# A three-block hybrid stack on one core: softmax start fused on VectorE, one attention step moved by a job, one weight split moved ahead of two squares

## The reference

```python
scores = einsum("bnqhgd,bnkhd->bhgnqk", qb, kb) * (HEAD_DIM ** -0.5)
scores = where(valid, scores + bias, NEG_INF)
m = maximum(max(scores, axis=-1, keepdims=True), sink_l)
p = exp(scores - m)
denom = sum(p, axis=-1, keepdims=True) + exp(sink_l - m)
p = p / denom
out = einsum("bhgnqk,bnkhd->bnqhgd", p, vb)
```

## Time and profile before

| what | value |
|---|---|
| median of three runs | 1438.81 us (1433.37 to 1439.4) |
| the profiled execution | 1435.38 us |
| its span, first to last instruction | 1433.6 us |
| mean granted TensorE clock | 0.985 |
| TensorE busy | 1364.9 us, 95% of the span |
| VectorE busy | 1027.4 us, 72% |
| ScalarE busy | 718.6 us, 50% |
| HBM read | 258.99 MB |

### The profile page before, as it was taken

How to read it: one execution, slowest core, us unless ns; L and a number is a source line. 1 busy time by engine, 2 the same in 40 slices (tenths; PEclk the granted TensorE clock), 3 DMA queues, 4 the chain that set the end, 5 groups by cost and what they waited for, 6 DMA issues and landing times. The chain is left out here.

```text
span 1433.6 us, 24250 instructions
## 1 busy us (share of the span) xinstructions
PE 1364.9 (95%) x9872; PEld 1260.0 (88%) x9872; DVE 1027.4 (72%) x1680; ACT 718.6 (50%) x1095; POOL 42.7 (3%) x80
## 2 busy tenths in 40 slices
PE   7999998999999999999998999999899999899996
PEld 6999997898999999999988989999778877889995
DVE  4487676776677664886777857777787986677775
ACT  5345657444443445446565443433468664545442
POOL 1000000000000000000000000000010000000000
PEclk9999999999999999999999999999999999999998
DMA  9964534463777654444444647677434313355450
GB/s 266 245 241 163 202 133 148 148 240 130 265 256 270 248 220 147 165 160 147 148 152 160 220 146 274 240 279 254 172 112 168 148 60 109 112 187 195 177 177 30
DMA packets 42152, 262.10 MB, mean 183 GB/s; under 512 B 5229, under 2 KB 5613, under 8 KB 14782
## 3 DMA queue, kind: packets, MB, share of 16 engines
q1 hardware_dynamic: 32688, 227.28, 45.5%
q0 software_dynamic: 9264, 33.24, 6.9%
q10 hardware_dynamic: 94, 0.07, 0.0%
HBM read 258.99 MB, written 1.58 MB: 182 GB/s over the span
## 5 line engine op out<-in xcount | busy, mean ns | idle before, releaser
L1608 DVE TENSOR_TENSOR split<-ring,split 128x1024 fp32r<-128x1024 f32 x412 | 487.3, 1220 | 204.8 <-ACT split L1165 203.9
L654 PE MATMUL psum<-h,split 128*128 128x256 f32 x2080 | 593.2, 285 | 6.9 <-DVE split L1608 6.4
L655 PE MATMUL psum<-h,split 128*128 128x256 f32 x2080 | 588.9, 283 | 0.0
L656 PE MATMUL psum<-h,split 128*128 128x256 f32 x2080 | 588.7, 283 | 0.0
L1165 ACT CAST split<-ring 128x1024 fp32r<-128x1024 f32 x411 | 410.5, 1047 | 254.0 <-PE psum L656 235.5
L654 PEld LDWEIGHTS psum<-h,split 128*128 128x128 f32 x2080 | 399.1, 192 | 19.9 <-issue 13.3
L655 PEld LDWEIGHTS psum<-h,split 128*128 128x128 f32 x2080 | 399.3, 192 | 1.0
L656 PEld LDWEIGHTS psum<-h,split 128*128 128x128 f32 x2080 | 399.3, 192 | 0.0
L654 PE MATMUL psum<-split,feed 128*128 128x512 f32 x296 | 118.0, 399 | 6.5 <-DVE feed L1608 4.1
L655 PE MATMUL psum<-split,feed 128*128 128x512 f32 x296 | 116.7, 394 | 0.0
L656 PE MATMUL psum<-split,feed 128*128 128x512 f32 x296 | 116.3, 393 | 0.0
(11 more groups left out here) (310 smaller groups left out, 1573.1 us busy)
## 6 DMA issues: line engine op xcount, KB each, us to landing
ring<-stream SPq DMA_DIRECT2D x213, 1024.0 KB, 4.9
arena<-ada POOLq DMA_DIRECT2D x48, 512.0 KB, 5.2
arena<-bias_by_distance POOLq DMA_DIRECT2D x8, 384.0 KB, 29.5
gain<-norm_rows POOLq DMA_DIRECT2D x4, 512.0 KB, 6.6
x<-x_in SPq DMA_DIRECT2D x2, 512.0 KB, 4.9
ring<-stream SPq DMA_DIRECT2D x2, 512.0 KB, 7.7
gain<-mod_rows POOLq DMA_DIRECT2D x2, 512.0 KB, 7.3
out<-x SPq DMA_DIRECT2D x4, 256.0 KB, 2.0
```

The source lines that it names most:

```text
L654: pe.matmul(out_, a[0], b[0], start=first, stop=False)
L655: pe.matmul(out_, a[0], b[1], start=False, stop=False)
L656: return pe.matmul(out_, a[1], b[0], start=False, stop=last)
L1608: return dve.tensor_tensor(out_, value, high.bitcast(F32), ALU.subtract)
```

## The change

Four edits, three of which move or replace work in the layers of the first block.

1. In `softmax_in`, the sum over both heads, the maximum and the maximum with the sink become one `tensor_tensor_reduce` per head: (scores + bias) x 1/8 written out, and the running maximum, which begins with the sink, in the accumulator.
2. So that the bias fits in before the scaling, the copy of the bias by distance at the start becomes an activation that multiplies by 8.
3. In layer 1 the first attention step stands at job c0 in place of `kd1`.
4. In job (wo,1) ScalarE splits the chunk of (wo,3) ahead of the two squares.

```diff
 ATT_LAYER = ([{k: i for i, k in enumerate(ATT_EARLY + [JOB["gp", 0] + i for i in range(8)])}]
-             + [{k: i for i, k in enumerate([JOB["kd", 1]] + ATT_EARLY + [JOB["gp", 0] + i for i in range(7)])}] * (L - 1))
+             + [{k: i for i, k in enumerate([JOB["c", 0]] + ATT_EARLY + [JOB["gp", 0] + i for i in range(7)])}] * (L - 1))
...
-                    act.copy(S1.rearrange("p u h s -> p (u h s)")[0:H1, 0:512], bank[4][0:H1, :]).then_inc(bias_sb, 1)
+                    act.activation(S1.rearrange("p u h s -> p (u h s)")[0:H1, 0:512], bank[4][0:H1, :], ACT.Copy,
+                                   scale=HD ** 0.5).then_inc(bias_sb, 1)
...
                     if name == "wo" and j == 1:
                         load_sqrt()
+                        next_high((l, "wo", 1))
                         square(2 * l + 1, "columns", 0)
                         square(2 * l + 1, "columns", 1)
...
-                    elif (name, j) not in (("wo", 3), ("gate", 0)) and name != "kd" and (l, name, j) not in AHEAD:
+                    elif (name, j) not in (("wo", 1), ("wo", 3), ("gate", 0)) and name != "kd" and (l, name, j) not in AHEAD:
                         next_high((l, name, j))
...
-                    stt(S1[:, u], psum[:, 4:6, 0:T], HD ** -0.5, bias_t[:, 2 * p:2 * p + 2, k0:k0 + T]).then_inc(s_read, 1)
+                    for hh in range(2):
+                        ins = dve.tensor_tensor_reduce(
+                            S1[:, u, hh, :], bank[4 + hh][:, 0:T], bias_t[:, 2 * p + hh, k0:k0 + T], HD ** -0.5,
+                            sink_sb[:, 2 * p + hh:2 * p + hh + 1], ALU.add, ALU.max, mx[:, u, hh:hh + 1])
+                    ins.then_inc(s_read, 1)
                     dve.wait_ge(s_read, l * UNITS1 + i + 1)
-                    link(dve.tensor_reduce(mx[:, u, :], S1[:, u], AX.X, ALU.max))
-                    link(dve.tensor_tensor(mx[:, u, :], mx[:, u, :], sink_sb[:, 2 * p:2 * p + 2], ALU.max))
```

## The result

| | median us | runs | ratio to before, 95% interval |
|---|---|---|---|
| before | 1438.81 | 5 (1433.37 to 1440.6) | |
| changed | 1423.91 | 5 (1422.71 to 1429.09) | 0.9906 [0.9887, 0.9925] |
| changed, second session | 1424.89 | 6 (1419.58 to 1431.79) | 0.9907 [0.9879, 0.9934] |

The change makes the kernel 0.94% faster, 13 to 15 us by the medians of the two sessions (the kernel before stood at 1437.95 in the second); the forecast was 1425.4. The profiled execution of the changed kernel took 1429.09 us, the slowest of its five.

What follows compares the result with a forecast made beforehand. The prediction took TensorE as the bound, with a closed loop of VectorE and ScalarE setting attention's tails. Its terms -3.2, -2.7 and -5.4 sum to -11.3 us, from 1435.4 to 1424.1, plus 1.3 gives 1425.4; range 1419 to 1434.

Steps and rivals of the forecast that it cites:

- What bounds the kernel: TensorE is busy 1364.9 of 1433.6 us; in attention's tails a closed loop of VectorE and ScalarE, 8.25 us per turn.
- Split before squares: Output product, both layers: TensorE's waits of 1.63 and 1.62 us go; -3.2 us, bounds 0 and -3.4.
- First step one job later: Layer 1's start: the 2.67 us wait for unit 0's scores goes; -2.7 us, bounds -2.7 and +0.5.
- The cover holds by 0.6 us at most: Layer 1, job c1: VectorE's split is ready at most 0.6 us early, and not without the fused instruction's gain.
- Fused instruction, 0.6 per unit: Softmax start: a pair of 1.0 us replaces 1.64; nine loop turns in the tails give -5.4 us.
- low bound of -7.5: Attention tails: the most the fused instruction's term was to gain, in us, if the clock improves as well.
- I count no gain of clock in the sum: Layer 1's tail: the clock falls to half for 6.7 us; no gain from its recovery was counted.
- the base of 1436.7: Mean in us of all four executions of the kernel before, 1.3 above the profiled one; the forecast added this 1.3.
- Half rate: Rival, softmax start: the fused pass runs at half rate, gaining only 0.15 us per unit; 1429.5 us, chance 0.15.
- The loop is no longer the bound: Rival, attention tails: TensorE's pace or ScalarE's copies take over, half the tail's gain is lost; 1428.1 us, chance 0.12.
- The split doesn't come earlier: Rival, output product: ScalarE waits at the moved split for load or buffer, -3.2 falls away; 1428.6 us, chance 0.06.
- A dear fused instruction: Rival: the pair takes x us more than 1.64, total -5.9 + 10x on 1436.7; 1446.8 at x 1.6, chance 0.05.

Runs made afterwards that it cites:

- e5: The changed kernel with a second pair of fused instructions ahead of the real one in every unit; 1434.29 us, ratio 0.9975 to the kernel before.
- e3: The kernel before with the fused sum, maximum and sink alone, in the old order; 1433.44 us, ratio 0.9963 to the kernel before.
- e4: The changed kernel with VectorE's softmax start ahead of the chunk's low halves in the gp jobs; 1423.31 us, ratio 0.9896 to the kernel before.
- e6: e4 with layer 0's softmax start of unit 15 also ahead of the gating of wp job 0; 1418.62 us, ratio 0.9864 to the kernel before.
- e1: The kernel before with only ScalarE's split of the output chunk moved ahead of the two squares; 1435.28 us, ratio 0.9976 to the kernel before.
- e2: The kernel before with only layer 1's first attention step moved one job later; 1435.87 us, ratio 0.9984 to the kernel before.

## Why the prediction was right, point by point

- **What bounds the kernel.** Right. The tails ran as a closed loop through VectorE's softmax start, and not at any engine's busy time. e5 shows it upward (turns 7.54 to 8.60), e3 downward and alone (8.25 to 7.54), e4 and e6 by opening it.
- **Split before squares, -3.2.** 3.64 in the stages, 3.3 alone. The mechanism was as drawn. The size was 0.2 us short in each layer, even beyond the bound of -3.4: I took the wait that the list shows (1.63), but when it goes everything behind moves by 1.82. In the timeline of before, matmuls of this form start 0.23 us apart; the two around the wait start at 322.43 and 324.44, 2.01 apart, 1.78 more than usual, and the next one another 0.34 later. So the wait in the list is shorter than the time that its going gives back; the list counts from modelled ends of matmuls to the next start.
- **First step one job later, -2.7.** 2.76 in the changed kernel. "The cover holds by 0.6 us at most" was right, and 0.44 to 0.48 by measurement; without the fused instruction it was gone, by 0.24 us. What the sum lacked is that the wait is sometimes followed by a stretch at half clock, 1.5 and 2.8 us in two of the three profiles that have it.
- **Fused instruction, 0.6 per unit, -5.4.** The instruction takes 479 ns, as the nearest row said. The term was mis-sized: the pair takes 0.92 us and not 1.0, so a unit gains 0.72 and not 0.6, and the turn is 7.54 and not 7.65. Nine turns of 0.71 are 6.4; the two tails gained 6.8, the rest came in layer 1, where the half clock went (next point). The low bound of -7.5 had no working behind it, and e3's tails passed it (8.3 us) by where the slow stretch fell. The bias scaled by 8 at the start shows no cost.
- **"I count no gain of clock in the sum."** In layer 1's tail the half clock of the earlier trace rows is gone (window of the changed kernel, with its clock of 1.00):

```profile
756.00:764.00 8.00, 7.94 (x65) 7.29 (x66) 7.67 (x15) 4.07 (x5) 0.00 (x0) 1.00 0.13 52
```

  Yet this stage gained 3.25, only 0.4 over four turns of 0.71. TensorE used to make up for its slow stretch with a shorter wait behind it: now two gaps (1.91 and 1.49 us between issues) stand where one of 4.02 and the slow stretch stood. While a loop sets the end, a slow TensorE inside it costs little. It is different once the loop is open (e6) or where nothing waits (the 4.2 us at 1170).
- **The sum.** Forecast -11.3, stages -13.2, medians -14.9 and -13.1. Each term was small by 0.1 to 1.4. That 1425.4 came within 1.5 us of the measured 1423.91 is in part luck: the base of 1436.7 was 1.3 to 2.4 us below the medians that the kernel before had in its four sets of runs (1437.95 to 1439.08), and the gain was put 1.9 us short of the stages', so the two errors cancel.
- **Rivals.** *Half rate* fell: 479 ns with PSUM, 482 with both operands in SBUF. The Trainium skill, "Vector Engine (DVE) Microarchitecture Reference", section 7, would have had the latter at half throughput; the trace of e5 doesn't agree with it for this instruction (both its operands were the same fp32 tile there, but the pass over 128x1024 with two different ones takes 1218 ns, as a plain one). *The loop is no longer the bound* fell, and became true with e4. *The split doesn't come earlier* fell with ScalarE's cast at 320.55. *A dear fused instruction* fell by its size, but its mechanism was real: a longer start lengthens each turn and breaks the cover of c1. Its formula gave 1435.6 for x = 0.48; with the measured 1.97 us in place of 1.64, x is 0.33 and the formula gives 1434.1, where e5 ran in 1434.29.

## What to carry to other kernels

When three engines go round in a loop, price an edit by its place in the turn times the number of turns, and ask of every instruction of the turn whether it has to be in it: moving 2.36 us of ready work out of the loop gained 4.2 us by stages on top of the fused instruction's 6.8, and in that order the fused instruction itself was worth 3 us and no longer 7, half of the 3 being clock. Judge gains of a few microseconds by stages between equal matmuls of two traces, and by many timed runs, since the spans of a single pair of profiles were off by 7 us here. A stage has its own noise, though: where a slow stretch can fall ahead of a wait or behind it, as in layer 0's tail, the same code differed by 1.5 us, and the point where the wait ends is the better mark. Where a wait of TensorE goes, expect a little more than the wait: its restart, and at times a stretch at half clock behind it.

## What was not expected of the hardware

- The second of two fused instructions starts 0.40 us after the first, although each takes 0.48, when nothing waits between them; with a semaphore wait between them it is 0.52 (1.05 for the extra pair of e5). The read of the accumulator (83 ns) is hidden in both cases.
- The same program, in the same stage, ran at full clock in one execution and at half clock for a while in another: 39.96 and 35.79 us for the same 188 matmuls near 1170. Which of the two an execution gets is left open here.
- The start of the program, its first 1577 matmuls, took 209.7 to 214.5 us over these twelve profiles. All of the difference lies in the first 600 of them, up to about 90 us; the other 977 take the same time in all profiles within 0.02 us. There the loads of chunks set the pace: the DMA engines are busy throughout (a share of 1.01 to 1.02 from 30 to 60 us in every profile), but moved 227 GB/s in that stretch in before's profile and 202 to 223 in the others. ScalarE's waits for a chunk from 20 to 90 us, in before and then in the changed kernel:

```profile
ACT split L1165 <- DMA ring<-stream: 16.4, 5, 5.6
```

```profile
ACT split L1165 <- DMA ring<-stream: 24.0, 6, 5.9
```

  They came to 21.7 to 24.7 us in all eleven profiles but before's. That an edit slows the loads is not shown: e1 and e2 change nothing so early and have it too, and the medians of the timed runs don't show the 4 us. Why the rate differs is left open.
